# GpSimd sums eight of the twelve w_mod units before TensorE takes them

## The reference, cut to what matters

```
mod_x = split(silu(c)     @ w_mod + b_mod, 6)    # w_mod is 1024 x 6144
mod_c = split(silu(c_ctx) @ w_mod + b_mod, 6)    # only parts 0 and 1 are used
```

## Time and profile before

| what | value |
|---|---|
| median of 3 runs | 1812.06 us (1811.24 to 1815.23) |
| the profiled execution | 1808.48 us |
| its span | 1806.6 us |
| PE busy | 1689.5 us (94%) |
| DVE busy | 661.4 us (37%) |
| ACT busy | 449.3 us (25%) |
| POOL busy | 170.4 us (9%) |
| chain that ended last, by engine | PE 76%, DMA 13%, DVE 6%, ACT 2% |
| granted TensorE clock, mean | 0.966 |

### The profile page before, as it was taken

One profiled execution on the slowest core, in us unless ns is written; L12 is line 12 of the kernel. 1 busy time (PEld: TensorE's weight loads), 2 busy tenths in 40 slices (PEclk: granted clock), 3 DMA queues, 4 the chain that ended last, 5 costly groups with the idle time before them and its releaser, 6 DMA issues.

```text
span 1806.6 us, 21815 instructions
## 1 busy us (share of the span) xinstructions
PE 1689.5 (94%) x8694; PEld 869.9 (48%) x8694; DVE 661.4 (37%) x1266; ACT 449.3 (25%) x807; POOL 170.4 (9%) x172
## 2 busy tenths in 40 slices
PE   7999999799999999999699998999799999999983
PEld 3455454445445555455345558965433333333331
DVE  3279341432122212122468946542522212221223
ACT  2233671233221112111448403332000000000002
POOL 0000000011111111110000013100111111111100
PEclk9999999799999999999899999999799999999997
DMA  9265531399999999999560181054799999999994
GB/s 363 102 238 183 199 129 47 127 397 402 401 401 405 409 403 399 402 413 413 194 246 1 21 128 48 1 208 194 270 396 398 405 408 407 404 420 409 418 417 183
DMA packets 94220, 515.26 MB, mean 285 GB/s; under 512 B 22429, under 2 KB 28157, under 8 KB 69544
## 3 DMA queue, kind: packets, MB, share of 16 engines
q1 hardware_dynamic: 82920, 496.46, 70.7%
q0 software_dynamic: 11200, 17.39, 2.9%
HBM read 506.09 MB, written 27.05 MB: 295 GB/s over the span
## 4 chain that ended last, share of the span: by engine, by line
PE 76%; DMA 13%; DVE 6%; ACT 2%; SPq 2%; issue 1%; DVEq 0%; POOLq 0%
PE bank L863 23%; PE bank L879 11%; PE bank L464 10%; PE bank L456 8%; DMA ring<-in_w_up 6%; DMA ring<-in_w_down 4%; PE bank L850 3%; PE bank L820 3%; PE bank L1232 3%; PE bank L890 2%; PE bank L522 2%; PE bank L687 2%; PE bank L449 1%; DVE arena L2608 1%; PE bank L729 1%
## 5 line engine op out<-in xcount | busy, mean ns | idle before, releaser
L865 PE MATMUL bank<-ring,arena 128*64 128x512 f32 x928 | 421.9, 609 | 0.0
L863 PE MATMUL bank<-ring,arena 128*64 128x512 f32 x752 | 339.4, 605 | 7.3 <-DMA ring<-in_w_up 4.7
L2507 DVE TENSOR_TENSOR arena<-arena,bank 64x512 f32<-64x512 f32 x70 | 48.3, 690 | 561.9 <-ACT arena L1801 561.9
L879 PE MATMUL bank<-ring,arena 128*64 128x512 f32 x544 | 248.0, 598 | 2.3 <-DMA ring<-in_w_down 2.3
L881 PE MATMUL bank<-ring,arena 128*64 128x512 f32 x544 | 247.9, 598 | 0.0
L456 PE MATMUL bank<-arena,ring 128*128 128x512 f32 x560 | 246.3, 596 | 0.0
L863 PEld LDWEIGHTS bank<-ring,arena 128*64 128x64 f32 x752 | 100.7, 139 | 207.0 <-issue 200.9
L863 PE MATMUL bank<-arena 128*64 128x512 f32 x368 | 167.4, 609 | 9.4 <-DMA ring<-in_w_up 5.7
L1801 ACT ACTIVATE arena<-bank 64x512 f32<-64x512 f32 x70 | 41.2, 589 | 512.7 <-PE bank L865 512.7
L1440 POOL DMA_INDIRECT arena<-xnd,smalli x70 | 67.7, 968 | 1058.3 <-PE bank L850 535.9
L456 PEld LDWEIGHTS bank<-arena,ring 128*128 128x128 f32 x560 | 105.8, 191 | 128.1 <-issue 128.1
(11 more groups left out here) (441 smaller groups left out, 1989.7 us busy)
## 6 DMA issues: line engine op xcount, KB each, us to landing
ring<-in_w_down SPq DMA_DIRECT2D x62, 2048.0 KB, 23.2
ring<-in_w_up SPq DMA_DIRECT2D x54, 2048.0 KB, 21.2
ring<-in_w_gate SPq DMA_DIRECT2D x45, 2048.0 KB, 13.4
arena<-in_w_gate SPq DMA_DIRECT2D x19, 2048.0 KB, 25.1
ring<-in_w_mod SPq DMA_DIRECT2D x12, 2048.0 KB, 15.2
ring<-in_w_in SPq DMA_DIRECT2D x10, 2048.0 KB, 17.3
arena<-in_w_up SPq DMA_DIRECT2D x10, 2048.0 KB, 29.3
ring<-in_w_out SPq DMA_DIRECT2D x4, 2048.0 KB, 11.2
```

The source lines that it names most:

```text
L863: pe.matmul(GU[0:CAP, :], x, wg_[:, c, :], start=(c == 0), stop=(c == KD - 1), skip_group_check=True)
L865: mm = pe.matmul(GU[CAP:2 * CAP, :], x, wu_[:, c, :], start=(c == 0), stop=(c == KD - 1), skip_group_check=True)
L879: pe.matmul(Y[0:CAP, :], x, wd_[:, c, 0:512], start=(c == 0), stop=(c == 3), skip_group_check=True)
```

## The change

Units 3, 4, 5, 6 and 9, 10, 11, 12 become summed ones. For each of them GpSimd, once the unit has landed, multiplies all 4096 columns in place by silu(c), broadcast from the column of each chunk, and then adds the upper half of the chunks onto the lower three times (2048, 1024 and 512 elements). What is left is one chunk whose sum over the partitions is the wanted row. TensorE takes it with four matmuls, whose stationary operand is a column of ones beside a column of zeros. The row of silu(c_ctx) isn't computed for these units. The four column blocks that need it are put on the units 7, 14, 15 and 16, which are still taken whole. The places of the units on TensorE and VectorE are moved too.

```diff
+        only_first = small(2)
-        for n, u in enumerate(U_MOD):
-            plain[u] = cols(a["w_mod"], n)
+        MOD = [4, 5, 6, 7, 0, 8, 9, 10, 11, 1, 2, 3]
+        SUMMED = [i for i, n in enumerate(MOD) if n >= 4]
+        for i, u in enumerate(U_MOD):
+            plain[u] = cols(a["w_mod"], MOD[i])
...
-            def modulation(n0, n1):
-                for n in range(n0, n1):
-                    w = use(U_MOD[n])
-                    b = V.deal(pe, f"mod{n}")
-                    for k in range(KD):
+            def modulation(*places):
+                for i in places:
+                    w = use(U_MOD[i])
+                    b = V.deal(pe, f"mod{MOD[i]}")
+                    if i in SUMMED:
+                        pe.wait_ge(S("mod_summed"), 4 * (SUMMED.index(i) + 1))
+                    for k in range(1 if i in SUMMED else KD):
                         for g in range(4):
-                            mm = pe.matmul(b[32 * g:32 * g + 2, 0:P], chunks(cs, 2)[:, k, :], w[:, k, P * g:P * g + P],
-                                           start=(k == 0), stop=(k == KD - 1), skip_group_check=True)
+                            c = only_first if i in SUMMED else chunks(cs, 2)[:, k, :]
+                            mm = pe.matmul(b[32 * g:32 * g + 2, 0:P], c, w[:, k, P * g:P * g + P], start=(k == 0),
+                                           stop=(i in SUMMED or k == KD - 1), skip_group_check=True)
...
-                    modulation(0, 5)
+                    modulation(0, 1, 2, 3, 4)
-            modulation(5, 9)
+            modulation(5)
-                    modulation(9, 10)
+                    modulation(6)
-                    modulation(10, 11)
+                    modulation(9)
-                    modulation(11, 12)
+                    modulation(7, 10)
+            modulation(8, 11)
...
-            sp.wait_ge(V.free, V.at("mod11"))
+            sp.wait_ge(V.free, V.at(f"mod{MOD[-1]}"))
...
+            pool.wait_ge(S("silu_c"), 1)
+            for n, i in enumerate(SUMMED):
+                pool.wait_ge(*landed(U_MOD[i]))
+                w = unit(U_MOD[i])
+                pool.tensor_tensor(w, w, chunks(cs, 2)[:, :, 0:1].to_broadcast([P, KD, 512]), ALU.mult)\
+                    .then_inc(S("mod_summed"), 1)
+                pool.wait_ge(S("mod_summed"), 4 * n + 1)
+                pool.tensor_tensor(w[:, 0:4, :], w[:, 0:4, :], w[:, 4:8, :], ALU.add).then_inc(S("mod_summed"), 1)
+                pool.wait_ge(S("mod_summed"), 4 * n + 2)
+                pool.tensor_tensor(w[:, 0:2, :], w[:, 0:2, :], w[:, 2:4, :], ALU.add).then_inc(S("mod_summed"), 1)
+                pool.wait_ge(S("mod_summed"), 4 * n + 3)
+                pool.tensor_tensor(w[:, 0, :], w[:, 0, :], w[:, 1, :], ALU.add).then_inc(S("mod_summed"), 1)
             experts(0)
...
+            dve.memset(only_first[:, 0:1], 1.0)
+            dve.memset(only_first[:, 1:2], 0.0).then_inc(S("consts"), 1)
```

More of the change, by code:

```diff
@@ L625, in context @@
                         four(CV, "SU", si, z[ZC[10]], z[ZC[6]])
-            def modulation(n0, n1):
-                for n in range(n0, n1):
-                    w = use(U_MOD[n])
-                    b = V.deal(pe, f"mod{n}")
-                    for k in range(KD):
+            def modulation(*places):
[5 more added lines that the diff above has]
+                    for k in range(1 if i in SUMMED else KD):
                         for g in range(4):
-                            mm = pe.matmul(b[32 * g:32 * g + 2, 0:P], chunks(cs, 2)[:, k, :], w[:, k, P * g:P * g + P],
-                                           start=(k == 0), stop=(k == KD - 1), skip_group_check=True)
+                            c = only_first if i in SUMMED else chunks(cs, 2)[:, k, :]
+                            mm = pe.matmul(b[32 * g:32 * g + 2, 0:P], c, w[:, k, P * g:P * g + P], start=(k == 0),
+                                           stop=(i in SUMMED or k == KD - 1), skip_group_check=True)
                     mm.then_inc(V.full, 1)
-                    used(U_MOD[n], V, f"mod{n}")
+                    used(U_MOD[i], V, f"mod{MOD[i]}")
             b = C.deal(pe, "ss_x")
-            pe.wait_ge(S("consts"), 3)
+            pe.wait_ge(S("consts"), 4)
             for k in range(0, KD, 2):
@@ L2155, in _, with modulation @@
             chain(TS(gq8, pcol("gq"), HD ** -0.5, None, ALU.mult))
-            def modulation(n0, n1):
-                for n in range(n0, n1):
+            def modulation(*places):
+                for i in places:
+                    n = MOD[i]
                     b = take(f"mod{n}")
```

## The result

| kernel | median, us | ratio to before, with its 95% interval |
|---|---|---|
| before, in the set of after | 1811.65 (4 runs) | 1 |
| after | 1871.53 (1868.19 to 1872.9, 4 runs) | 1.0322 [1.0303, 1.0342] |

The change makes the kernel 59.9 us slower; 1882 was forecast, inside 1845 to 1900. The profiled execution of after took 1870.96 us, its span is 1868.8, and its mean granted clock is 0.948.

The account below looks back on a forecast made before the run. PE was taken as the bound, taking turns with VectorE in the changed stage. `pw` 67 us late plus 4 of clock gave +71 on 1808.5, 1879.5; with the runs' median 3.6 above, 1882 was forecast, range 1845 to 1900.

Parts of the forecast that it names:

- The rule: While GpSimd works, VectorE gets one SBUF instruction in after each of GpSimd's, which last up to 7.6 us; chance 0.6.
- The first rival: SBUF port shared, not held: VectorE keeps 35% of its rate, `pw` at 247, 1865 us; chance 0.18.
- The second: VectorE wins the port and GpSimd stands still: taps on time, sums late, `pw` at 227.6, 1846 us; chance 0.12.
- The third: VectorE's taps don't collide with GpSimd: `pw` 2 us earlier, 1810 us, or 1799 at best; chance 0.1.
- The first half: Units 3 to 6, up to `qk4`: the copy of `qk0` comes 15.3 us late, `qk4` at 133.6.
- The second half: Units 9 to 12, after `qk4`: GpSimd works until 211, 16 VectorE instructions let in, `dwconv` at 241.6 instead of 176.0.
- From `dwconv` to `pw`: PE's column sums, units and value tiles from `mu` to `pw` take 23.4 us: `pw` at 265, +67 us.
- The saving: PE's shorter units, without any effect on VectorE: `pw` at 195.8 instead of 198.1, about 2 us saved.
- The sum: Whole kernel: 67 + 4 = +71 us on the profiled execution's 1808.5, giving 1879.5.
- the clock's 4 us: PE's lower clock after two waits on the path, at 104 and at `mu`, 2.2 us a restart: +4.

Follow-up runs that it names:

- Experiment 2: Changed kernel with each GpSimd instruction replaced by a memset of the same tile, which reads no SBUF: 1878.44 us against 1810.56 for before, ratio 1.0374.
- experiment 5: Changed kernel with the same sums cut into GpSimd instructions of 512 elements, 120 instead of 32: 1852.63 us against 1811.36 for before, ratio 1.0224.
- experiment 1: Changed kernel without GpSimd's 32 instructions and PE's wait for them, places and short units kept: 1811.10 us against 1810.56 for before, ratio 0.9999.
- experiments 7 to 10: Kernel before with VectorE's w_mod copies earlier (7, ratio 0.9999), with units 3 and 4 summed as well (8, 0.9962; 10, 0.9956), or those sums alone (9, 0.9990).

## Why the prediction was right

**The rule.** One instruction of VectorE's with two SBUF inputs after each of GpSimd's: the whole loss rests on it, and it held to the instruction (15 and 15). Experiment 2 shows that it is GpSimd's reads, and experiment 5 that the length of GpSimd's instructions counts, as whole instructions would have it. The first rival would have put `pw` at 247 and left experiment 5 where after is. The second, where GpSimd stands still and the taps are on time, is contradicted by the normalisation of 7.39 us, beside which GpSimd's product lost 0.45. The third, no collision, by taps of up to 7393 ns.

**The first half.** Forecast: `qk0`'s copy 15.3 us late and PE idle as long. Measured: 97.37, 8.6 late, and PE idle 9.05. The term was mis-sized: a unit of GpSimd's was set at 16.5 us from the earlier trace rows, and is 15.3 (7.02, 4.50, 2.35 and 1.27, and gaps). Unit 5's product ends at 75.0, not 79.2, so L2234 (L2211 before) waits only for that unit's long add and is over at 80.4, where the forecast had it wait for all the adds, until 87.1. L2236 and L2237 then wait for the very instructions that were named, the product and the long add of unit 6, which end at 90.9 and 96.4 instead of 96.8 and 102.8. Four units end at 101.1, not 108.5. The figure of 4497 ns that the prediction gave from the Trainium skill (GPSIMD Engine Reference, "3.1 Elementwise — side-by-side cycle accounting") is that of the row at 59.77, 4.50 us. The sum by it would have been closer. `qk4` was still near the forecast (131.1 for 133.6), by a second error: it was taken to be late by the shift of `ss_qk0` alone. But PE runs slowly after the wait: 2.05 for 1.02, 9.08 for 7.03, and 3.59 for 2.03 at the fifth unit, 4.6 us together. That is 8.3 + 4.6 = 12.9.

**The second half.** Forecast: GpSimd from 134.5 to 211, 16 of VectorE's instructions let in, `dwconv` at 241.6. Measured: 130.9 to 197.2, 15 let in, 228.6. Of the 13 us, 3.6 are the earlier start and 10.1 the units' length (66.3 us for four instead of 76.4), less 0.8 for the one turn fewer. There each unit loses 1.45 us to VectorE (16.75 for 15.3), not 2.6: an instruction let in costs GpSimd some 0.35 us (7.47 for 7.02, 4.82 for 4.50), not 0.65. The rule was right in who waits, and too strict in how long GpSimd does. What follows, 52 less the let-in ones at 0.775 us, came as worked out.

**From `dwconv` to `pw`.** Forecast 23.4 us and 2 of clock; measured 26.5, since `mu` takes 3.75 instead of 1.88 and the next unit 2.93 instead of 1.93: 2.9 us of the lower clock, where 2.2 were reckoned for a restart.

**The saving.** The 2 us that PE's shorter work was to bring don't exist: in experiment 1 `pw` is 0.9 us later. The idle time that it leaves costs the clock in what comes next.

**The sum.** 1879.5 was worked out for the profiled execution, 1870.96 measured. `pw` was to be 67 us late and was 57.2: 13.0 too much at `dwconv`, 3.1 too little behind it. With the clock's 4 us, which the sum adds to the 67, the stage was put 13.8 us too high. Behind `pw` the shift passed to the end, as costed, and `w_out` wasn't waited for; but another 5.0 us came up there (62.2 at the span's end), for which the sum has no term. That the total is only 8.5 us off is in part luck: two errors of opposite sign.

## What to carry to other kernels

Work given to GpSimd isn't free because GpSimd is idle: while it reads SBUF, VectorE gets one instruction with two SBUF inputs in for each of GpSimd's, so long GpSimd instructions beside a chain of short DVE ones are the worst case seen here. Put it where VectorE is idle, or bound by PSUM reads, reciprocals or waits; if it must overlap, cut it into instructions as short as VectorE's. And take work off an engine only together with the wait behind it: here less work on PE, and earlier copies on VectorE, brought nothing that can be told alone, and 0.4% together, of which 2 us are seen in the stage.

## What the runs showed of the hardware

- The turns aren't even in cost. A tap that waits for its turn takes up to 7.39 us; GpSimd loses 0.32 to 0.45 us for it, and 0.85 for a DVE instruction of 1024 elements (5.35 for 4.50 at 91.01).
- A TENSOR_SCALAR in SBUF waits for GpSimd's reads too: 2.20 us for 0.69 at 78.21.
- GpSimd's broadcast product of 4096 elements takes 7.02 us (1.71 ns each), an add with two full inputs of 2048 takes 4.50 (2.20 ns each), a memset of 4096 takes 3.52.
- PE pauses in some runs of short matmuls (two columns stationary), in the middle of a unit, with nothing to wait for that the profile shows: 1.20 to 1.91 us in before and in experiments 7 to 10, after 50 to 258 records in a row. Not every run has one: the 256 records at 106.99 in before have none. The cause is open.
